# Cast and low part of an attention's output one item later in the queues, and low parts of the blocks ahead of a weight split

## The reference, cut to what matters

```python
def step(qi):
    s = jnp.einsum('bqhgd,bkhd->bhgqk', qi, k).astype(jnp.float32) * scale
    p = jax.nn.softmax(s, axis=-1).astype(v.dtype)
    return jnp.einsum('bhgqk,bkhd->bqhgd', p, v)
...
out = _block_attention(q[:, :, :, None], k_all, v_all, scale) @ w_o
```

```python
blk = kv[:, cmp_idx] + pos[None, None, :, None, :]
blk = jnp.moveaxis(blk, 3, 2).reshape(B_, n_cmp, G, CMP_BLOCK * dh)
return jax.nn.gelu(blk @ w1) @ w2
```

## Time and profile before

| | |
|---|---|
| median of 3 runs | 2292.64 us (2291.72 to 2293.32) |
| the profiled execution, its own time | 2289.91 us |
| its span, first to last instruction | 2288.1 us |
| mean granted TensorE clock | 0.993 of full speed |
| busy: TensorE, weight loads, VectorE, ScalarE | 98%, 87%, 78%, 51% of the span |
| instructions | 37319 |

### The profile page before, as it was taken

The page is one execution under the profiler, slowest core; times in us unless marked ns, Lnnn a source line. Parts: engine busy times, 40 slices in busy tenths (PEclk is TensorE's granted clock), DMA queues, the critical chain, the costliest instruction groups (busy, mean ns, idle before and its releaser), DMA issues.

```text
span 2288.1 us, 37319 instructions
## 1 busy us (share of the span) xinstructions
PE 2239.3 (98%) x14860; PEld 1990.3 (87%) x14860; DVE 1788.3 (78%) x3510; ACT 1168.5 (51%) x2110; POOL 0.2 (0%) x4
## 2 busy tenths in 40 slices
PE   8999999999999999999999999999999999998998
PEld 7878889898899988897988987798888889978998
DVE  7788977789887898878898765477877876477888
ACT  4685554665544555458655544534212236375433
POOL 0000000000000000000000000000000000000000
PEclk9999999999999999999999999999999999999999
DMA  7316666356565566650665532024554523324563
GB/s 245 134 63 221 235 195 217 121 208 234 189 217 175 206 235 194 212 191 20 230 231 191 177 111 74 1 74 150 172 175 158 173 80 112 128 80 147 197 230 127
DMA packets 70157, 373.54 MB, mean 163 GB/s; under 512 B 7392, under 2 KB 16736, under 8 KB 37984
## 3 DMA queue, kind: packets, MB, share of 16 engines
q1 hardware_dynamic: 61472, 361.52, 46.2%
q10 hardware_dynamic: 8512, 9.63, 1.4%
HBM read 369.03 MB, written 1.05 MB: 162 GB/s over the span
## 4 chain that ended last, share of the span: by engine, by line
PE 85%; DVE 9%; ACT 3%; DMA 2%; issue 1%; ACTq 0%; DVEq 0%
PE ps L483 80%; DVE w_lo L1783 3%; PE ps L808 2%; PE ps L791 1%; DMA w_raw<-weights 1%; PE ps L746 1%; ACT hid_f L1373 1%; DVE hid_f L2173 1%; DVE hid_f L2188 1%; ACT w_hi L1173 1%; PE ps L736 1%; DVE v_sb L2287 0%; DVE ps L1817 0%; DVE X L2056 0%; DVE hid_both L1783 0%
## 5 line engine op out<-in xcount | busy, mean ns | idle before, releaser
L483 PE MATMUL ps<-a_both,w_hi 128*128 128x256 f32 (+1 forms) x4864 | 1188.6, 330 | 18.5 <-DVE a_both L1840 10.4
L483 PEld LDWEIGHTS ps<-a_both,w_hi 128*128 128x128 f32 x4864 | 809.4, 190 | 96.3 <-issue 15.3
L483 PE MATMUL ps<-a_both,w_lo 128*128 128x256 f32 (+1 forms) x3136 | 886.7, 292 | 0.0
L1783 DVE TENSOR_TENSOR w_lo<-w_raw,w_hi 128x1024 fp32r<-128x1024 f32 (+1 forms) x632 | 707.8, 1148 | 86.7 <-ACT w_hi L1173 79.8
L483 PEld LDWEIGHTS ps<-a_both,w_lo 128*128 128x128 f32 x3136 | 596.0, 190 | 26.5
L483 PE MATMUL ps<-hid_both,w_hi 128*128 128x512 f32 (+2 forms) x2216 | 602.8, 351 | 8.7 <-issue 4.5
L1173 ACT CAST w_hi<-w_raw 128x1024 fp32r<-128x1024 f32 (+1 forms) x448 | 414.7, 974 | 373.0 <-DMA w_raw<-weights 371.8
L483 PEld LDWEIGHTS ps<-hid_both,w_hi 128*128 128x128 f32 x2216 | 387.7, 190 | 66.7 <-issue 7.6
L483 PE MATMUL ps<-hid_both,w_lo 128*128 128x256 f32 (+2 forms) x1460 | 439.4, 305 | 0.0
L483 PEld LDWEIGHTS ps<-hid_both,w_lo 128*128 128x128 f32 x1460 | 277.5, 190 | 14.4
L1179 ACT CAST w_hi<-w_raw 128x1024 fp32r<-128x1024 f32 (+2 forms) x184 | 187.7, 1020 | 2.6 <-DMA w_raw<-weights 2.6
(11 more groups left out here) (235 smaller groups left out, 1957.0 us busy)
## 6 DMA issues: line engine op xcount, KB each, us to landing
w_raw<-weights SPq DMA_DIRECT2D x250, 1024.0 KB, 4.8
pe_sb<-weights SPq DMA_DIRECT2D x96, 512.0 KB, 5.6
w_raw<-weights SPq DMA_DIRECT2D x64, 704.0 KB, 4.0
pe_sb<-na_bias ACTq DMA_DIRECT2D x32, 128.0 KB, 2.1
X<-x_t SPq DMA_DIRECT2D x2, 512.0 KB, 6.8
X<-c_rows ACTq DMA_DIRECT2D x2, 512.0 KB, 4.6
qk<-qk ACTq DMA_DIRECT2D x4, 256.0 KB, 6.7
qk<-ctx_t ACTq DMA_DIRECT2D x1, 1024.0 KB, 5.4
```

The lines of the kernel that those rows point to most:

```text
L483: return nc.tensor.matmul(out, stationary, moving, start=start, stop=stop)
L1783: return v.tensor_tensor(out, a, b.bitcast(F32), ALU.subtract)
```

## The change

In the attention, ScalarE's cast of a finished output moves from the step in which the item is 3 back to that in which it is 4 back, and VectorE's low part from 4 back to 5 back; both loops get one step more. TensorE's program is not touched, and neither is any wait. In `run_nsa`, VectorE makes the low parts of the second half of the blocks ahead of `skip("")`, that is ahead of the split of the weights of compress 1/0, and not behind it.

```diff
--- before.py
+++ after.py
@@ -1338,7 +1338,7 @@
 
             def attention(name):
                 a, items = att[name], ITEMS[name]
-                for i in range(len(items) + 3):
+                for i in range(len(items) + 4):
                     if i < len(items):
                         act.wait_ge(a["s_taken"], i + 1)
                         for r, (c, _) in enumerate(items[i]["rows"]):
@@ -1352,7 +1352,7 @@
                         if b >= 2:
                             act.wait_ge(a["pv_done"], b - 1)
                         nc.scalar.copy(t_ring[:, b % 2, :], ps[:, T0 + b % 2, :]).then_inc(a["t_taken"], 1)
-                    b = i - 3
+                    b = i - 4
                     if 0 <= b and items[b]["last"]:
                         act.wait_ge(a["pv_done"], b + 1)
                         t = items[b]["tile"]
@@ -2207,7 +2207,7 @@
             def attention(name):
                 a, items = att[name], ITEMS[name]
                 tiles = 0
-                for i in range(len(items) + 4):
+                for i in range(len(items) + 5):
                     if i < len(items):
                         dve.wait_ge(a["s_ready"], i // 2 + 1)
                         if i >= 4:
@@ -2225,7 +2225,7 @@
                         for r, (c, _) in enumerate(items[b]["rows"]):
                             last = v.tensor_scalar(p_slot[b % 4][:, c], p_slot[b % 4][:, c], recip[:, b % 4, r:r + 1], None, ALU.mult)
                         last.then_inc(a["p_ready"], 1)
-                    b = i - 4
+                    b = i - 5
                     if 0 <= b and items[b]["last"]:
                         tiles += 1
                         dve.wait_ge(a["o_hi"], tiles)
@@ -2327,8 +2327,8 @@
                 skip("")
                 ahead(scaled_unit(queries(3)))
                 step(v.memset(vg_hi.bitcast(F32), 0.0))
+                blocks_low(1)
                 skip("")
-                blocks_low(1)
                 ahead(keys(0))
                 step(v.memset(vg_lo.bitcast(F32), 0.0))
                 skip("")
```

## The result

The changed kernel takes 2304.33 us in the median of 5 runs (2300.03 to 2307.17), the kernel before 2292.12 us (2290.64 to 2293.32, 5 runs): a ratio of 1.0053, 95% interval [1.0042, 1.0064], or 12.2 us slower. The profiled execution took 2306.01 us, 16.1 us more than that of before; so it is one of the longer of the five, and what its trace shows is more than the median loses.

The account below looks back on a forecast made before the run. TensorE, busy 98% of the span, was taken to bound the kernel. Attention waits of +11.25 us and -2.33 us in the NSA blocks sum to +8.9 us on the median 2292.64: 2301.5 us, range 2296.7 to 2306.2.

Parts of the forecast that it names:

- waits 0.3 us longer than worked out: Attention, upper bound: each of the six waits 0.3 us longer, 13.0 us in place of 11.25.
- rival D: NSA blocks: the moved low parts give nothing because keys 1 are late; +11.25 us, 2303.9 us; chance 15%.
- The chain: Attention, head-pair changes: transposes, copy, cast, low part run serially before the product, 2.64 us; three changes cost +11.25 us.
- VectorE's own steps: Attention: taking scores and normalizing ahead of the low part are no later than the cast, so add nothing.
- The end of the stage: Attention, behind the last tiles: no copy left between, last casts wait only for TensorE; costs nothing more.
- the clock: TensorE in the attention: gaps of 2.0 and 2.1 us do not lower the granted clock; priced at nothing.
- a granted clock under 1.00 in the attention: Sign in the changed profile's attention that would show the prediction wrong.
- Rival C: Attention: the clock falls after each head-pair change, 2.4 us each, 7.3 us in all, 2308.8 us; chance 6%.
- Edit 2: NSA blocks: low parts fit VectorE's idle time, closing TensorE's gaps; gain 1.25 and 1.08 us, together -2.33 us.
- keys 1: Unit after compress 1/0 in the NSA blocks, next that could be late; its weights come out ahead, if barely.
- A: Attention, first product with V of tiles 2 to 7: wait hidden, gaps of 0.38 us close; -3.4 us, 2289.2; 4%.
- B: Attention: only odd tiles or a shorter chain count, 6.4 us or less, full NSA gain; +4.1 us, 2296.7; 10%.

Follow-up runs that it names:

- Edit 1 alone: Kernel before with only the attention's cast and low part one item later, NSA blocks as before: 2306.36 us against 2291.72, ratio 1.0065.
- the fillers: Changed kernel plus six unneeded TensorE matmuls ahead of each of the six waiting products: 2299.60 us, ratio 1.0033 to the kernel before.
- edit 2 alone: Kernel before with only the NSA blocks' second-half low parts moved ahead of the weights' split, attention as before: 2288.89 us, ratio 0.9985.
- the cast alone: Kernel before with only ScalarE's cast one item later, VectorE's low part in its old step: 2309.39 us, ratio 1.0072.

## Why the prediction was right

**The size and the side.** 2301.5 was forecast, in a range of 2296.7 to 2306.2, and 2304.33 measured. Against its own median of before the forecast was +8.9 us, the measurement +12.2. That the time lies within the range owes something to luck. The upper end of the range (2305.6 + 0.7, which is 2306.3) was made of waits 0.3 us longer than worked out and of no gain in the NSA blocks; neither came. What filled that room is a term that the sum had at nothing. The measured time also lies beside rival D's 2303.9, and D's mechanism did not happen either.

**The chain, term by term.** 0.70 + 0.48 + 0.62 + 0.84 = 2.64 us came out as 0.70, 0.48, 0.62 and 0.84 at the first tile, and as 2.63 in all at the odd one. Every move of an instruction in a queue was followed to the product that waits, and the six waits of 1.98 us are the 2.0 and 2.1 of the text. VectorE's own steps were no later than the cast, as said. The end of the stage cost nothing more. Added up, the six products start 11.2 us later, for 11.25 forecast. Edit 1 alone shows that sum with a remainder: 14.6 us in the median, 15.7 in the attention of its profiled execution.

**The step that was mis-sized is the clock.** "so by the nearest row I price the clock at nothing", with 1.85 us of idle at full clock as that row. The prediction named "a granted clock under 1.00 in the attention" as a sign of being wrong, and it is there: 0.90. The remainder of 3 to 4 us is that term: 12.2 less (11.25 - 2.8) is 3.7, and the fillers, which leave the chain as it is, take 4.3 us away. Rival C, given 6% and +7.3 us, is what happens, in a smaller size in the median and in full in the profiled execution: 18.9 us less the 11.2 us by which the six products start later is 7.7 us. What misled is that one gap of one execution was taken for the rule. The same gap late in the kernel stands in every profile, and in that of the run with cast and low part early the clock falls behind it:

```profile
2133.24 0.50 PE L483 MATMUL ps<-a_both,w_hi 128*128 128x256 f32 x2 [1.83 <-DVE a_both L1783]
```

```profile
2134.70:2138.00 3.30, 3.30 (x16) 2.96 (x15) 0.87 (x3) 1.05 (x4) 0.00 (x0) 0.50 0.00 0
```

It falls there in 3 of the 11 profiled executions: in two behind 1.83 us, and with six fillers behind 2.41 us, to which that gap had grown. In the other eight, at 1.83 to 1.85 us, the clock stays at 1.00. So the row of the prediction was one draw of two outcomes, and "nothing" was the more frequent of them at this place; in the attention, at 1.98 us, the other one is more frequent. Why that is so, and whether it matters that these gaps come in twos, some 6 to 8 us apart and each behind transposes, is not shown. The Trainium skill ("TensorE: Matmul & The Clock Gate", "HAM oscillation — how this bites in real kernels") tells of a kernel in which the lower clock comes back behind every wait. The trace agrees in kind, with five of six waits, but the waits of that kernel are of about 3 to 5 us, and the section says nothing of 1.98 us; that by its rule the sum would be rival C's took it further than it goes.

**Edit 2.** -2.33 us forecast, -2.8 measured (interval -5.5 to -1.4 us), and locally 1.25 us in the first block, as forecast. The hole on VectorE was as read, keys 1 were in time (the low part of their weights starts at 62.36 with edit 2 alone, its first half takes 1.2 us, and TensorE takes it up at 63.71, so it was as close as the prediction said), and rival D fell. The spacing of 0.12 us between matmuls that the gain was worked out with stands in the rows (61.78, 61.90).

**The other rivals.** A asked for the low part to be ready before the product; no run of the changed order comes near it, but the runs with the early order do, and gain what A gave for it and a little more (1.8 for 1.1 us). B, the shorter chain with a gain from elsewhere, has no row for it.

## What to carry to other kernels

A wait that is hidden by one item of lead turns into the whole chain when the lead is given up: before moving an instruction back in a queue, write down which instruction stands ahead of it in the new place, and whether that one waits for the same engine which will wait for you. Move such hand-backs of a PSUM bank towards the idle time of their engine, ahead of the next item's work, not behind it. And when gaps of about 2 us open on TensorE again and again, add the lower clock behind them as a term with both ends, here from nothing to some 1.5 us for each gap, even if one gap of about this length elsewhere in the trace cost nothing. One row shows one outcome; look for the same gap in as many executions as there are.

## What was not expected of the hardware

- Gaps of 1.98 us, two at each change of head pair, lowered the granted clock to 0.50 for 3.4 us behind five of the six; gaps of 1.19 us at the same places did not. With 1.68 and 1.50 us it fell behind one of six. The single gap of 1.85 us late in the kernel, which cost nothing in the kernel before, lowered the clock for 3.4 us in two other executions, at 1.83 us. A gap of this size is not needed either: with edit 2 alone the clock was at 0.50 from 2082.6 to 2086.0 us behind gaps of 0.49 and 0.36 us.
- Which of the gaps lower the clock differs between executions: five stretches in the attention of the changed kernel (17 us), three with edit 1 alone, four with the cast alone, though the six waits are of 1.98 us in all three. What decides is not known. The five runs of the changed kernel order by their mean clock: 2300.03 us at 0.992, 2301.91 at 0.991, 2304.33 and 2306.01 at 0.990, 2307.17 at 0.989. Outside the attention it varies too: around the gap of 4.48 us the lower clock lasted 6.8 us in the profiled execution of before (2105.6 to 2112.4), and behind the same gap of the changed kernel (4.51 us) it lasted 3.4 us.
- Matmuls that nobody needs made a kernel 4.3 us faster in the median. With them in the wait, the product also started 0.75 us after its last input's start (1430.54 to 1431.29) in place of 0.84, at six places 0.5 us; why it starts sooner is not known.
